# Gate and up stages of a two-layer encoder: the norm factor moved from the operand blocks to the results of each strip

## The reference, cut to what matters

```python
def _rmsnorm(x, g):
    xf = x.astype(jnp.float32)
    y = xf * lax.rsqrt(jnp.mean(xf * xf, axis=-1, keepdims=True) + RMS_EPS)
    return (y * g.astype(jnp.float32)).astype(x.dtype)
...
def _swiglu(h, w_gate_up, w_down):
    gu = h @ w_gate_up
    g, u = jnp.split(gu, 2, axis=-1)
    return (jax.nn.silu(g) * u) @ w_down
...
        h = _rmsnorm(x, norm_ffn[i])
        x = x + _swiglu(h, ffn_w_gate_up[i], ffn_w_down[i]).astype(x.dtype)
```

## Time and profile before

| | |
|---|---|
| time before, median of 3 runs | 2284.55 us (2279.5 to 2284.84) |
| the profiled execution | 2281.84 us, its span 2279.8 us |
| PE busy | 2206.7 us, 97% of the span |
| DVE busy | 1354.9 us, 59% |
| ACT busy | 905.7 us, 40% |
| POOL busy | 671.6 us, 29% |
| mean granted TensorE clock | 0.989 of full speed |

### The profile page before, as it was taken

The page is one execution under the profiler, slowest core; times in us unless marked ns, Lnnn a source line. Parts: engine busy times, 40 slices in busy tenths (PEclk is TensorE's granted clock), DMA queues, the critical chain, the costliest instruction groups (busy, mean ns, idle before and its releaser), DMA issues.

```text
span 2279.8 us, 32796 instructions
## 1 busy us (share of the span) xinstructions
PE 2206.7 (97%) x11320; PEld 1801.1 (79%) x11320; DVE 1354.9 (59%) x2073; ACT 905.7 (40%) x1602; POOL 671.6 (29%) x487
## 2 busy tenths in 40 slices
PE   7998898999999999999999999999799999999998
PEld 6876686888888888877888777778688888888887
DVE  5658568655554588447332467746865555458842
ACT  4017444333333344332221477744433333334433
POOL 2523322322222053120000266642232222205312
PEclk9999998999999999999999999999999999999999
DMA  6430440433332673233443777744043333267312
GB/s 226 107 99 13 139 153 32 139 101 120 101 120 83 204 240 111 78 98 120 144 152 101 214 176 179 170 139 154 31 140 101 120 101 120 83 216 231 111 47 88
DMA packets 268899, 290.68 MB, mean 128 GB/s; under 512 B 16512, under 2 KB 221568, under 8 KB 264592
## 3 DMA queue, kind: packets, MB, share of 16 engines
q1 hardware_dynamic: 257808, 249.68, 36.8%
q10 hardware_dynamic: 11008, 39.92, 4.5%
HBM read 200.50 MB, written 81.85 MB: 124 GB/s over the span
## 4 chain that ended last, share of the span: by engine, by line
PE 88%; DVE 6%; DMA 3%; SPq 1%; POOL 1%; ACT 1%; issue 1%; ACTq 0%; DVEq 0%; POOLq 0%
PE psum L2191 12%; PE psum L2195 12%; PE psum L2193 12%; PE psum L1921 7%; PE psum L1922 7%; PE psum L1923 7%; PE psum L2249 4%; PE psum L2253 4%; PE psum L2251 4%; PE psum L2069 3%; PE psum L2094 3%; PE psum L2169 2%; PE psum L2170 2%; PE psum L2171 2%; PE psum L2029 1%; PE psum L2030 1%
## 5 line engine op out<-in xcount | busy, mean ns | idle before, releaser
L2191 PE MATMUL psum<-b_hi,a_hi 128*128 128x512 f32 x1232 | 484.1, 393 | 21.6 <-DVE b_lo L1601 20.5
L2193 PE MATMUL psum<-b_lo,a_hi 128*128 128x512 f32 x1232 | 482.2, 391 | 0.0
L2195 PE MATMUL psum<-b_hi,a_lo 128*128 128x512 f32 x1232 | 482.0, 391 | 0.0
L2191 PEld LDWEIGHTS psum<-b_hi,a_hi 128*128 128x128 f32 x1232 | 233.1, 189 | 73.2 <-issue 25.1
L2195 PEld LDWEIGHTS psum<-b_hi,a_lo 128*128 128x128 f32 x1232 | 233.0, 189 | 49.0
L2193 PEld LDWEIGHTS psum<-b_lo,a_hi 128*128 128x128 f32 x1232 | 233.2, 189 | 48.7 <-issue 0.5
L888 POOL TENSOR_TENSOR a_sum<-a_raw 128x512 f32<-128x512 f32 x88 | 115.3, 1310 | 499.2 <-DVE a_lo L1596 442.5
L854 POOL TENSOR_TENSOR score<-score,inv_l 128x128 f32<-128x128 f32 (+7 forms) x128 | 144.9, 1148 | 349.6 <-DVE inv_l L1482 347.8
L1921 PE MATMUL psum<-h_hi,w_hi 128*128 128x512 f32 x544 | 214.3, 394 | 5.3 <-DVE w_lo L1389 3.0
L1923 PE MATMUL psum<-h_hi,w_lo 128*128 128x512 f32 x544 | 213.0, 391 | 0.0
L1922 PE MATMUL psum<-h_lo,w_hi 128*128 128x512 f32 x544 | 212.7, 391 | 0.0
(11 more groups left out here) (230 smaller groups left out, 4262.3 us busy)
## 6 DMA issues: line engine op xcount, KB each, us to landing
a_raw<-in_ffn_w_gate_up SPq DMA_DIRECT2D x88, 512.0 KB, 5.1
hid_scr<-hid_out SPq DMA_DIRECT2D x44, 512.0 KB, 5.7
x_t<-x_scr SPq DMA_DIRECT2D x16, 1024.0 KB, 7.1
t_scr<-t_out SPq DMA_DIRECT2D x16, 1024.0 KB, 6.1
d_full<-t_scr SPq DMA_DIRECT2D x16, 1024.0 KB, 5.8
x_scr<-x_t ACTq DMA_DIRECT2D x24, 512.0 KB, 2.7
d_full<-hid_scr SPq DMA_DIRECT2D x12, 1024.0 KB, 9.1
w_raw<-in_fox_w_in SPq DMA_DIRECT2D x22, 512.0 KB, 4.0
```

Of the source, the lines that this page charges most:

```text
L2191: T.matmul(out_ps, a_hi[i][:, j, :], b_hi[i][:, j, :], start=not more and j == 0, stop=False, skip_group_check=True)
L2193: T.matmul(out_ps, a_hi[i][:, j, :], b_lo[i][:, j, :], start=False, stop=False, skip_group_check=True)
L2195: last = T.matmul(out_ps, a_lo[i][:, j, :], b_hi[i][:, j, :], start=False, stop=j == KH - 1, skip_group_check=True)
```

## The change

The blocks are formed without the norm factor, straight from the residual: gain times x, by ScalarE (a copy with a scale, `scaled`) or by VectorE (gain times x minus another block, in one scalar_tensor_tensor, `minus_part`). They no longer wait for the factor. The factor `rstd_gu` (a copy of `rstd_ffn` at another place) is multiplied into four results of each strip: the two halves of the gate before Silu, and the two halves of up.

With it, VectorE forms block 2 and most of block 4 in the last but one column strip of the out-projection; ScalarE forms the high parts of blocks 1 and 5; the spreading of the factor comes later in TensorE's order; Silu's table is loaded ahead by a one-column instruction; and since `rstd_gu` lies where features 6 and 7 of `x_t` lie, pair 3 of the residual is loaded last but one and pair 2 first.

```diff
-        n00, n10, n01 = [at(f"n{w}", k0, [P, KH, HALF]) for w, k0 in (("00", 124), ("10", 132), ("01", 92))]
-        n11 = b_full[5]
+        n00 = at("n00", 124, [P, KH, HALF])
+        b_full[4] = at("b_full4", 132, [P, KH, HALF])
+        rstd_gu = at("rstd_gu", 24, [P, SEQ])
...
-        D_PAIRS = (3, 0, 1, 2)
+        D_PAIRS = (2, 0, 1, 3)
...
-                load_x(3)
+                load_x(2)
                 store_hid(layer, FT - 2, 0)
                 sp.wait_ge(a_low, NP * (last + 1))
                 for w in range(2, 4):
                     load_even(0, w)
-                load_x(2)
                 for n in range(4):
                     load_block(n)
...
                 store_hid(layer, FT - 1, 1)
                 load_x(0)
+                load_x(3)
                 for q in range(2):
                     sp.wait_ge(hid_stored[q], 16 * (FT // 2 * (layer + 1)))
                 load_x(1)
...
+                    if j == KD + 3:
+                        scaled(n00, k, 0, 0).then_inc(n_done, 1)
                     if j == KD + 4:
-                        block_high(layer, 0)
+                        block_high(layer, k, 0)
                     if j == KD + 5:
-                        block_high(layer, 1)
+                        block_high(layer, k, 1)
...
+            def scaled(dst, k, kh, h):
+                for j in range(KH):
+                    m = KH * kh + j
+                    last = nc.scalar.activation(dst[:, j, :], x_t[:, m, half(h)], ACT.Copy, scale=gains[:, k, m:m + 1])
+                return last
...
+                if i == 1:
+                    scaled(b_hi[1], k, 1, 0).then_inc(b_high, 1)
+                    return
+                if i == 5:
+                    act.wait_ge(t_dve, 4 * layer + 4)
+                    act.wait_ge(b_low, NP * layer + 5)
+                    scaled(b_hi[5], k, 1, 1).then_inc(b_high, 1)
+                    return
...
             def ffn(layer, c0, k):
                 r0 = FT * layer
+                for i in (2, 3, 4):
+                    block_high(layer, k, i)
+                weight_high(r0 + 1, 1, 0)
                 norm_root(k, 1)
-                for i in range(2):
+                weight_high(r0 + 1, 1, 1)
+                keep_first(r0, 0)
+
+                nc.scalar.activation(warm[:, :], eps_c[:, :], ACT.Silu)
+                for i in (5, 6):
+                    block_high(layer, k, i)
+                for i in (2, 3):
                     weight_high(r0 + 1, 1, i)
                 norm_spread(k, 1)
-                for i in range(2, NP):
-                    block_high(layer, i)
+
+                act.wait_ge(b_low, NP * layer + 6)
+                act.wait_ge(x_stored, 16 * (2 * KD * layer + KD + 1))
+                act.wait_ge(rstd_ready, 2 * k + 2)
+                nc.scalar.activation(rstd_gu[:, :], rstd_ffn[:, :], ACT.Copy).then_inc(rstd_moved, 1)
                 products_act(r0, 0, True)
...
-                    if j == KD + 3:
-                        dve.wait_ge(rstd_ready, 2 * k + 1)
-                        normed(layer, k, n00, 0, 0)
-                    if j == KD + 4:
-                        normed(layer, k, n10, 1, 0)
                     if j == KD + 5:
-                        block_low(layer, 0, n00)
+                        block_low(layer, k, 0)
                     if j == KD + 6:
-                        block_low(layer, 1, n10)
+                        block_low(layer, k, 1)
+                    if j == 2 * KD - 2:
+                        dve.wait_ge(evac_done, 2 * (c0 + j) + 2)
+                        first_minus(b_full[2], k, 0, n00, range(KH))
+                        dve.wait_ge(t_dve, 4 * layer + 1)
+                        for i in range(KH - 1):
+                            minus_part(b_full[4], k, 1, 1, b_full[2], i)
+                    if j == 2 * KD - 1:
+                        dve.wait_ge(evac_done, 2 * (c0 + j) + 2)
+                        minus_part(b_full[4], k, 1, 1, b_full[2], KH - 1).then_inc(t_dve, 1)
...
+            def minus_part(dst, k, kh, h, other, j):
+                m = KH * kh + j
+                return V.scalar_tensor_tensor(out=dst[:, j, :], in0=x_t[:, m, half(h)], scalar=gains[:, k, m:m + 1],
+                                              in1=other[:, j, :], op0=ALU.mult, op1=ALU.subtract)
...
+                if i in (1, 5):
+                    for j in range(KH):
+                        last = minus_part(b_lo[i], k, 1, 0 if i == 1 else 1, high_part, j)
...
+            def blocks_dve(layer, k):
+                dve.wait_ge(n_done, layer + 1)
+                dve.wait_ge(t_dve, 4 * layer + 2)
+                V.tensor_tensor(b_full[3][:, :, :], b_full[4][:, :, :], n00[:, :, :], ALU.subtract).then_inc(t_dve, 1)
+                block_low(layer, k, 2)
+                block_low(layer, k, 3)
+                for i in range(2):
+                    weight_low(FT * layer + 1, 1, i)
+                block_low(layer, k, 4)
+                dve.wait_ge(b_low, NP * layer + 3)
                 for j in range(KH):
+                    last = minus_part(b_full[6], k, 1, 0, b_full[4], j)
+                last.then_inc(t_dve, 1)
+                norm_diag(k, 1)
+                block_low(layer, k, 5)
+                block_low(layer, k, 6)
+                for i in (2, 3):
+                    weight_low(FT * layer + 1, 1, i)
...
+                def by_norm(x, h, n):
+                    dve.wait_ge(c_raw, 4 * r + n)
+                    V.tensor_tensor(x, x, rstd_gu[:, half(h)], ALU.mult).then_inc(c_done, 1)
...
-                V.tensor_tensor(gate_h[0], bk(1), p1_keep[:, :], ALU.add).then_inc(c_done, 1)
...
+                V.tensor_tensor(gate_h[0], bk(1), p1_keep[:, :], ALU.add).then_inc(c_raw, 1)
+                if not last and not first:
+                    weight_low(r + 1, 1 - q, 1)
+                by_norm(gate_h[0], 0, 1)
...
                 product(r0, 0, 1, b0)
-                norm_bc(k, 1)
                 for i in range(2):
                     product(r0 + 1, 1, i)
                 for i in range(2, NP):
                     product(r0, 0, i, b0)
+                    if i == 3:
+                        norm_bc(k, 1)
+
+                pe.wait_ge(rstd_ready, 2 * k + 2)
                 for i in range(2, NP):
                     product(r0 + 1, 1, i)
```

More of the change, by code:

```diff
@@ L1597, in weight_low @@
                     .then_inc(a_low, 1)
-            def block_low(layer, i, src):
-                dve.wait_ge(b_high, NP * layer + i + 1)
-                V.tensor_tensor(b_lo[i][:, :, :], src[:, :, :], b_hi[i][:, :, :].bitcast(FP32), ALU.subtract)\
-                    .then_inc(b_low, 1)
-            def normed(layer, k, dst, kh, h):
-                for j in range(KH):
-                    m = KH * kh + j
-                    last = V.scalar_tensor_tensor(out=dst[:, j, :], in0=x_t[:, m, half(h)],
-                                                  scalar=gains[:, k, m:m + 1], in1=rstd_ffn[:, half(h)],
-                                                  op0=ALU.mult, op1=ALU.mult)
-                last.then_inc(n_done, 1)
@@ new lines, in first_minus, with block_low @@
+            def first_minus(dst, k, kh, other, js):
+                for j in js:
+                    last = minus_part(dst, k, kh, 1, other, j)
+                last.then_inc(t_dve, 1)
+            def block_low(layer, k, i):
+                dve.wait_ge(b_high, NP * layer + i + 1)
+                high_part = b_hi[i][:, :, :].bitcast(FP32)
+                if i in (1, 5):
+                    for j in range(KH):
+                        last = minus_part(b_lo[i], k, 1, 0 if i == 1 else 1, high_part, j)
+                else:
+                    if i == 4:
+                        dve.wait_ge(nat_done, NORM_SEQ[k, 1])
+                    last = V.tensor_tensor(b_lo[i][:, :, :], (b_full[i] if i else n00)[:, :, :], high_part, ALU.subtract)
+                last.then_inc(b_low, 1)
@@ L1696, in products_dve @@
                 wait(dve, hid_done, 2 * (r - 1))
-                V.tensor_tensor(gate_h[0], bk(1), p1_keep[:, :], ALU.add).then_inc(c_done, 1)
-                if not last:
-                    if not first:
-                        weight_low(r + 1, 1 - q, 1)
+                V.tensor_tensor(gate_h[0], bk(1), p1_keep[:, :], ALU.add).then_inc(c_raw, 1)
+                if not last and not first:
+                    weight_low(r + 1, 1 - q, 1)
+                by_norm(gate_h[0], 0, 1)
+                if not last and not first:
                     weight_low(r + 1, 1 - q, 2)
@@ L1706, in products_dve @@
                 V.tensor_tensor(p57_keep[:, :], bk(3), p5_keep[:, :], ALU.add).then_inc(p57_kept, 1)
-                if not last:
+                if not last and not first:
                     weight_low(r + 1, 1 - q, 3)
-                else:
+                elif last:
                     down_weight_low(layer, 0)
@@ L1748, in ffn @@
                 r0 = FT * layer
-                norm_diag(k, 1)
```

(3 more changed lines are left out.)

57 lines of the change are left out of this document (22 added, 35 removed).

## The result

The changed kernel takes 2287.77 us (median of 20 runs, 2281.45 to 2295.05) against 2282.36 us for the kernel before on the same chip (median of 20, 2275.86 to 2289.4). The ratio is 1.0025, 95% interval 1.0013 to 1.0036: slower by some 5.7 us. That is less than the 0.3% that the prediction took as the least it could tell from no change, but the interval lies wholly above 1. The prediction was 2285.0 us, with 2273 to 2296 as its range. The profiled execution of the changed kernel took 2292.16 us, its span 2290.1 us; it is one of the longer of the twenty.

A forecast was written before the change was run, and what follows sets the result against it. VectorE was taken to bound the entries into the gate and up stages. Entries -2.1 and -0.5, catching up +0.5 and down stage +2.5 sum to +0.4 us, put on the median 2284.55: 2285.0 us, range 2273 to 2296 (8 in 10).

The forecast's parts named there:

- What bounds: Entries into gate and up stages: VectorE sets their end, not TensorE; six waits on `b_lo` there, 20.5 us.
- The new wait: TensorE's sums for the norm, behind the last strip's delayed addition: a stall of 7.9 us, bounds 1.5 and 7.9.
- the turn: End of the out-projection: five GpSimd additions put themselves between VectorE's eleven instructions, each for 1.27 us.
- Rival 1: Entries: GpSimd's turns cost little, the gate comes 6.4 us sooner in each layer, 2272.2 us; chance 0.24 with its mixtures.
- Product 5: Entry: starts 35.8 us after product 0, behind a 3.3 us wait; -2.1 us in layer 0, -0.5 in layer 1.
- rival 2: TensorE's clock falls after product 5 (+5.8) and at the down stage (2 x 2.5): 2295.8 us; chance 0.21 with mixtures.
- The factor in the strips: Gate and up strips: four multiplications make VectorE 13.4 of 19.0 us busy; costed at nothing in the steady strips.
- The 0.5 us for catching up in strips 1 and 2: Just after the entry VectorE is late at `p5_keep`: 0 to 2 us for both layers together, 0.5 taken.
- The down stage: Changed order of x loads makes pair 1 late: 1.0 us in layer 0, 1.5 in layer 1, +2.5; bounds 0 and +9.3.
- the first block comes 3.0 us sooner: Down stage: without 1 MB of `x_t` ahead, its load comes 3.0 us sooner; no sooner would show the prediction wrong.
- the last `hid`: Down stage: ready about when it was, VectorE's 3.0 us earlier start paying for three queued multiplications (1.9).
- the emptier queue: Down stage loads: gives back part of the 3.0 us that the megabyte ahead of pair 1 costs; half taken, 1.5.

The follow-up runs named there:

- the run with the sums early: Changed kernel with GpSimd's four weight sums of strip 1 moved to column strips 9 to 12 of the out-projection: 2281.16 us, ratio 1.0 against the kernel before.
- second profile: The changed kernel run once more with no edit, for another profile; the two profiled executions differ by 10.3 us.

## Why the prediction was right, and where its terms were not

**What bounds.** Right: VectorE's queue. With the largest wait taken away TensorE waited 8.84 us elsewhere, and P5 moved by 1 us; with VectorE's queue 4.2 us shorter P5 moved by 4.8 and 4.2. But for product 5 the order on ScalarE counts too: with the copy to `p5_keep` ahead of Silu E came 3.4 us sooner and 1.7 of them stayed.

**The new wait.** Right in kind and near in size: 6.7 us for 7.9. The term that was too large is the turn, 1.05 us instead of 1.27. I took it between the 1.03 that four instructions felt of one addition and half of a pair; the first was the measurement of the thing itself. The Trainium skill (SBUF — State Buffer, "SBUF: two separate sides") calls the ports an exclusive lock; the timelines agree in kind, with the addition that of two full queues neither keeps it. In size the turn is less than the whole of the other instruction: a GpSimd addition took 1.28 us where VectorE had nothing beside it (331.50 in the run with the sums early), and costs VectorE 1.05. Rival 1 is out.

**Product 5.** Forecast 35.8 us behind product 0 with a wait of 3.3 ahead of it; 36.2 and 35.7 with 3.5. At the upper clock the entry is 41.5 us against 43.4 and 41.9 before, -1.9 and -0.4 for -2.1 and -0.5 forecast. But the 43.4 holds 1.55 us of the lower clock. The sum set a layer before with the slow product 4 against a layer after without a slow product. With both at the upper clock the change wins 0.4 us a layer.

**The clock** is the term that I left to a rival. Behind that gap the entry lost 2.7 us in layer 0 and 1.3 in layer 1 (44.27 and 42.84 less 41.53), and products 5 and 6 took 8.09 and 7.16 us in place of 5.55. That half of rival 2 came true and turned the entries' gain of 2.3 us into a loss of 1.8 in the first profile, and of 0.3 in the second (+0.9 and -0.6). Rival 2 held that a slow stretch is hidden where VectorE is the bound. Before, it fell on product 4, and only about half of it was hidden: product 4 took 2.5 us longer, and P5 came 1.2 us later than in layer 1.

**The factor in the strips.** Right: 394.40 us with and without it. But the reasoning, 13.4 of 19.0 us, promised 5.6 us of room, which is eight more instructions of 0.7. One more was nearly free, and three more cost 1.9 us a strip (39.1 us between E and D, some 21 strips). So that the four cost nothing was partly luck: the busy share did not show how near the limit was. The 0.5 us for catching up in strips 1 and 2 was nothing.

**The down stage** was mis-sized: 5.3 us more of waits against 2.5 forecast, inside the 0 to 9.3. Two steps failed. First, "the first block comes 3.0 us sooner": counted from D its low part came 0.4 and 1.5 us sooner, and SyncE issued its load no sooner at all in layer 0 (13.5 us ahead of D in both kernels: at 774.20 before and at 772.63 after), which the prediction itself had named as a sign of being wrong. 1.2 of that is the `hid` store of the last strip but one, delayed by its multiplications, behind which the blocks' loads stand on SyncE's queue. I had followed the multiplications of the last strip only. Without the factor the gain is 2.2 us in layer 0 and 2.7 in layer 1, near the 3.0. Secondly, the last `hid` was not ready when it had been before, but 2.1 us later in layer 0 and 1.0 in layer 1. And the emptier queue gave nothing back. DMA share between 790 and 797, the kernel before and the kernel after:

```profile
790.00:797.00 7.00, 7.00 (x32) 5.81 (x31) 6.87 (x10) 2.20 (x4) 0.00 (x0) 1.00 1.18 300
```

```profile
790.00:797.00 7.00, 7.00 (x32) 5.82 (x31) 6.23 (x11) 2.20 (x4) 0.63 (x1) 1.00 0.83 203
```

The x loads could not use the free time, as they stand behind the second store, which started at 796.56. So the megabyte ahead of pair 1 made VectorE's third addition 2.5 and 2.9 us later, near all of its 3.0, and not half.

**The sum.** Forecast -2.1 - 0.5 + 0.5 + 2.5 = +0.4. Measured, with the entries after at the upper clock: -1.9 - 0.4 + 0 + 5.3 = +3.0, and the clock adds 2.6 (second profile) to 4.1 us (first): 5.6 to 7.1, near the 5.7 us of the ratio. So the change cost some 5 us more than forecast, by two terms: the down stage (2.8 too small) and the clock, put at nothing in the sum. The time came out only 2.8 us over the forecast, because the median of the kernel before lay 2.2 us lower in these 20 runs than in the three shown. That part of the agreement is luck.

## What to carry to other kernels

Moving a factor from operands to results cost nothing here where the results are made, as VectorE's queue had room, and was paid at the two ends of the stage: the first result that a product waits for, and the last store that loads stand behind. Follow each added instruction to the last strips' stores and to what is queued behind them. The room of a queue is not the idle share: look at the waits inside its chains and the turns with the other engine, and measure the room by doubling instructions, several of them and in several places. Before a gain is put down to a change, compare entries at the same clock.

## What the runs showed of the hardware

A GpSimd addition of 128x512 in float32 puts itself between two VectorE instructions that read both inputs from SBUF, for 1.05 us each time, one against one for as long as both have a queue (343.85 to 352.3 above, and 4.2 us back when four were moved). Such an addition took 1.28 us with VectorE idle beside it.

After gaps of equal length TensorE's next product ran at the lower of its levels (1.2 GHz, matmuls 0.43 us apart) in some executions and at the upper (2.4 GHz, 0.23 apart) in others. At the same place of the same program, product 5 of layer 1 behind 3.48 and 3.49 us, it fell to the lower level after six matmuls in one execution and not at all in the other. Over the five profiles with a gap of 3.45 to 3.50 us ahead of product 5 the lower level followed in five of ten cases, four of them in layer 0. So such a gap is worth its own 3.5 us and, in about half of the cases seen here, up to 2.7 us more, which is to be seen only in several profiles.
